# First expert's turned rows from an early gather of five tiles and one-hot products, in a decoder layer on one core

## What is computed

```python
x = x + merged @ w_out[l]
h2 = rms_norm(x, norm2_g[l])
x = x + hier_moe(h2, ...)
...
gl = (hf @ w_gr + b_gr)                     # 4 groups
g_idx = jnp.argmax(gl, axis=-1)
el = (hf @ w_er + b_er).reshape(N, N_GROUPS, EXPERTS_PER_GROUP)
top_v, top_i = lax.top_k(el_sel, TOP_K)     # 2 of the 8 experts of the group
w = jax.nn.softmax(top_v, axis=-1) * p_g[:, None]
...
a = xb @ w_gate[eid]
u = xb @ w_up[eid]
(jax.nn.silu(a) * u) @ w_down[eid]          # for each expert, on the rows that chose it
out = jnp.zeros((N, D)).at[row_tok].add(ys * row_w[:, None])
```

## Time and profile before

| | before |
|---|---|
| median of 3 runs | 1482.31 us (1481.53 to 1482.49) |
| the profiled execution: its time | 1481.47 us |
| the profiled execution: its span | 1479.7 us |
| TensorE busy | 1424.3 us, 96% of the span |
| VectorE, ScalarE, GpSimd busy | 1008.1, 828.9, 407.7 us |
| granted TensorE clock, mean | 0.99 |
| DMA, mean | 194 GB/s; 375 to 396 GB/s from slice 25 of 40 to slice 39 |

### The profile page before, as it was taken

The page is one execution under the profiler, slowest core; times in us unless marked ns, Lnnn a source line. Parts: engine busy times, 40 slices in busy tenths (PEclk is TensorE's granted clock), DMA queues, the critical chain, the costliest instruction groups (busy, mean ns, idle before and its releaser), DMA issues.

```text
span 1479.7 us, 19519 instructions
## 1 busy us (share of the span) xinstructions
PE 1424.3 (96%) x7296; PEld 1199.5 (81%) x7297; DVE 1008.1 (68%) x1444; ACT 828.9 (56%) x1342; POOL 407.7 (28%) x462
## 2 busy tenths in 40 slices
PE   5899999999999999999999979999999999999996
PEld 5788888888888788888888867888888888888885
DVE  6855664664574533344332567999999999999996
ACT  5653453353353322233232227888888888888883
POOL 3225424424433400000000011233333333333331
PEclk9999999999999999999999988999999999999999
DMA  7010110210210143354330549999999999999992
GB/s 220 23 44 12 51 44 1 62 43 1 61 44 0 44 115 99 86 149 121 91 142 36 198 152 385 375 386 385 392 386 387 386 389 389 393 396 393 389 384 89
DMA packets 134032, 286.39 MB, mean 194 GB/s; under 512 B 18864, under 2 KB 97840, under 8 KB 109360
## 3 DMA queue, kind: packets, MB, share of 16 engines
q1 hardware_dynamic: 119216, 263.79, 49.3%
q0 software_dynamic: 13248, 21.00, 3.8%
q10 hardware_dynamic: 1472, 0.32, 0.1%
HBM read 287.16 MB, written 25.17 MB: 211 GB/s over the span
## 4 chain that ended last, share of the span: by engine, by line
PE 85%; DMA 4%; DVE 4%; ACT 2%; POOL 2%; issue 2%; POOLq 0%; DVEq 0%; ACTq 0%
PE proj L105 17%; PE proj L107 16%; PE proj L106 16%; PE scores L105 6%; PE scores L107 6%; PE scores L106 6%; DMA w_slot<-in_w_up 4%; PE outs L760 2%; PE scores L693 2%; PE scores L571 1%; PE turned L105 1%; PE turned L107 1%; PE turned L106 1%; PE outs L851 1%; DVE w_low L1747 1%
## 5 line engine op out<-in xcount | busy, mean ns | idle before, releaser
L1747 DVE TENSOR_TENSOR w_low<-w_slot,w_high 128x2048 fp32r<-128x2048 f32 x192 | 430.9, 2285 | 0.1
L1186 ACT ACTIVATE w_high<-w_slot 128x2048 fp32r<-128x2048 f32 x190 | 352.6, 1907 | 20.1 <-DMA w_slot<-in_w_up 8.5
L105 PE MATMUL proj<-w_high,xeH 128*128 128x512 f32 x512 | 203.8, 398 | 3.9 <-DVE xeL L1850 1.9
L107 PE MATMUL proj<-w_high,xeL 128*128 128x512 f32 x512 | 200.6, 392 | 0.0
L106 PE MATMUL proj<-w_low,xeH 128*128 128x512 f32 x512 | 200.1, 391 | 0.0
L1376 POOL DMA_INDIRECT out<-y,ids_rows x31 | 86.5, 2791 | 342.8 <-DVE y L1860 342.8
L999 ACT ACTIVATE wCH<-wC_in 128x1024 fp32r<-128x1024 f32 x48 | 47.6, 1052 | 154.1 <-DMA wC_in<-in_w_branch_b 154.1
L1442 DVE TENSOR_TENSOR wCL<-wC_in,wCH 128x1024 fp32r<-128x1024 f32 x48 | 56.9, 1237 | 92.3 <-ACT wCH L999 92.3
L105 PEld LDWEIGHTS proj<-w_high,xeH 128*128 128x128 f32 x512 | 97.0, 189 | 25.5 <-issue 3.7
L107 PEld LDWEIGHTS proj<-w_high,xeL 128*128 128x128 f32 x512 | 96.5, 188 | 20.9
L106 PEld LDWEIGHTS proj<-w_low,xeH 128*128 128x128 f32 x512 | 96.7, 189 | 19.2
(11 more groups left out here) (299 smaller groups left out, 3167.4 us busy)
## 6 DMA issues: line engine op xcount, KB each, us to landing
w_slot<-in_w_gate SPq DMA_DIRECT2D x64, 1024.0 KB, 11.1
w_slot<-in_w_up SPq DMA_DIRECT2D x64, 1024.0 KB, 11.2
w_slot<-in_w_down SPq DMA_DIRECT2D x64, 1024.0 KB, 11.7
wC_in<-in_w_in SPq DMA_DIRECT2D x32, 512.0 KB, 4.8
wB_in<-in_w_in SPq DMA_DIRECT2D x16, 512.0 KB, 6.1
wA_in<-in_w_in SPq DMA_DIRECT2D x12, 512.0 KB, 5.9
x_all<-in_x SPq DMA_DIRECT2D x4, 1024.0 KB, 8.8
wC_in<-in_w_branch_a SPq DMA_DIRECT2D x16, 256.0 KB, 5.7
```

The lines of the kernel that those rows point to most:

```text
L105: pe.matmul(out, lh, rh, start=start, stop=False)
L107: return pe.matmul(out, ll, rh, start=False, stop=stop)
L1186: act.activation(w_high[slot][:], w_in6[slot][:], ACT.Copy).then_inc(S["w_split"], 1)
L1747: dve.tensor_tensor(w_low[slot][:], w_in6[slot][:], w_high[slot][:].bitcast(F32), ALU.subtract).then_inc(S["w_lows"], 1)
```

## The change

`first_ids`: when the positions of tiles 0 to 4 are known, their part of the table of rows is summed on its own. VectorE keeps it (in `w_rows`) and writes the first expert's column as `first_ids`. GpSimd gathers these rows of the first five tiles into `xe1`, ahead of its work on the norm of tile 6, as soon as the first five tiles are stored. Rows of later tiles stay zero there.

`first_pick`: for tiles 5, 6 and 7 VectorE writes a one-hot of the position within the first expert (`first_hot`; `far` moves tokens of other experts out of range). TensorE multiplies slices of `x2` with it (`first_late`), adds the early rows by products with the identity (`first_early`), and so has the first expert's turned rows in two PSUM banks without a full gather. VectorE scales them (`first_scaled`), ScalarE copies the first four slices one by one, and the first piece's products wait for each slice (`low_of`).

Moved: `picks` of tiles 5 to 7 and the last `rows_of` go behind the first slices and the first weight piece (`last_rows` on TensorE); the tables, and with them the gathers of `xe0` and `xe1`, come after that. `top_group` has six operations in place of seven. The third weight piece is split within the projection (ScalarE behind half 11, VectorE behind tile 2's placing), the fourth behind the second half's copy. `first_sq` keeps its place ahead of pieces 4 and 5, and now waits for the later gather. SyncE issues pieces 4 to 7 without a hold, and 8 and 9 once `x2` is no longer read.

```diff
@@ SyncE
             load_piece(3)
             store_x2(N_TILES - 1)
-            sp.wait_ge(S["xe_landed0"], DMA)
             for q in range(4, 6 * N_EXP):
                 if q == 8:
-                    sp.wait_ge(S["x2_stored"], N_TILES * DMA)
-                    sp.wait_ge(S["out_stored"], N_TILES * DMA)
+                    sp.wait_ge(S["x0_T"], 2)
+                    sp.wait_ge(S["early_stored"], 2 * N_EARLY * DMA)
+                    sp.wait_ge(S["late_stored"], 2 * (N_TILES - N_EARLY) * DMA)
                 load_piece(q)
@@ TensorE
+            def first_late(t, ks):
+
+                pe.wait_ge(S["place_step"], FIRST_HOT[t])
+                for k in ks:
+                    last = pe.matmul(first_turned(k), x2[:, t, DS(k, 128, step=8)], first_pick[t - N_EARLY][:, :],
+                                     start=(t == N_EARLY and k % 4 == 0), stop=(t == N_TILES - 1 and k % 4 == 3))
+                return last
+
+            def first_early(ks):
+
+                pe.wait_ge(S["xe_landed1"], DMA)
+                for k in ks:
+                    pe.matmul(first_turned(k), xe[1][:, DS(k, 128, step=8)], ident, start=False, stop=False)
+
+            first_late(5, range(4))
             turn_half(15)
+            first_late(5, range(4, 7))
+            positions_of(6)
             route_half(15)
-            positions_of(6)
-            rows_of(5)
+            first_early(range(4))
+            first_late(6, range(4))
+            first_late(5, [7])
+            first_early(range(4, 8))
             positions_of(7)
-            rows_of(6)
-            rows_of(7)
...
+            first_late(6, range(4, 6))
+            first_late(7, range(4)).then_inc(S["x0_T"], 1)
+            first_late(6, range(6, 8))
+            first_late(7, range(4, 8)).then_inc(S["x0_T"], 1)
...
-            pe.wait_ge(S["xe_landed0"], DMA)
-            for half, done in ((0, "x0_T"), (1, "xeT_done")):
-                for k in range(4 * half, 4 * half + 4):
-                    last = pe.transpose(SC[:, 0, k * 128:(k + 1) * 128], xe[0][:, DS(k, 128, step=8)], ident)
-                last.then_inc(S[done], 1)
@@ ScalarE
-                if cnt in (9, 10):
+                if cnt in (9, 10, 11):
                     high(w_high[cnt - 9][:], w_in6[cnt - 9][:], S[f"w_land{cnt - 9}"], DMA, S["w_split"])
...
-            high_piece(2)
+            act.wait_ge(S["xs_done"], 4)
+            for k in range(4):
+                act.activation(xeH[:, k, :], xs[:, k, :], ACT.Copy).then_inc(S["x0_H"], 1)
+            act.wait_ge(S["xs_done"], 8)
+            act.wait_ge(S["route_step"], R_DIFFS)
+            act.activation(xeH[:, 4:8, :], xs[:, 4:8, :], ACT.Copy).then_inc(S["xeH_done"], 1)
             high_piece(3)
-            act.wait_ge(S["route_step"], R_DIFFS)
...
             act.wait_ge(S["xe_landed0"], DMA)
+            act.wait_ge(S["rows_mm"], 9)
             act.activation(first_sq[:], xe[0][:], ACT.Square, scale=1.0 / 32, accum_out=first_ms[:]).then_inc(S["first_sum"], 1)
@@ GpSimd
             for i in range(N_TILES):
+                if i == N_EARLY + 1:
...
+                    pool.wait_ge(S["early_stored"], 2 * N_EARLY * DMA)
+                    pool.wait_ge(S["tables_done"], 1)
+                    pool.indirect_dma_start(out=xe[1][:], out_offset=None, in_=x2_dram[0:N_EARLY * 128, :],
+                                            in_offset=bass.IndirectOffsetOnAxis(ap=first_ids[:, 0:1], axis=0),
+                                            bounds_check=N_EARLY * 128 - 1, oob_is_err=False).then_inc(S["xe_landed1"], DMA)
@@ VectorE
+            def first_hot(t):
+
+                dve.wait_ge(S["pos_mm"], t + 1)
+                place(dve.scalar_tensor_tensor(first_pick[t - N_EARLY][:], pos_bank(t)[:, 0:1].to_broadcast([P, 128]),
+                                               far[:, t - N_EARLY:t - N_EARLY + 1], const("iota", 0, 128), ALU.add, ALU.is_equal))
...
+                if i == 7:
+                    first_hot(5)
+                    place_rows(5)
                 add_residual(1, i)
...
+                if i == 6:
+                    dve.wait_ge(S["rows_mm"], N_EARLY)
+                    route(dve.tensor_scalar(w_rows[:, 0:32], bank(3)[:, 0:32], float(NO_ROW), None, ALU.add))
+                    row_ids(first_ids[:], bank(3)[:, 0:1], "tables_done")
```

More of the change, by code:

```diff
@@ L32 @@
 DMA = 16
[L35 removed]
+R_DIFFS, R_WEIGHTS = 86, 103
 NO_ROW = 1024
@@ L38 @@
 N_GROUPS = 4
+NO_SLOT = 4096.0
+N_EARLY = 5
+PLACED = {t: 2 * t + 2 + max(t - N_EARLY + 1, 0) for t in range(N_TILES)}
+FIRST_HOT = {t: PLACED[t] - 2 for t in range(N_EARLY, N_TILES)}
 def expert_at(j):
@@ L305, in decoder_layer @@
         r_rows = rs("r_rows", [P, 256])
+        first_pick = [sb(f"first_pick{i}", [P, 128], F32, at=R_WORK + 16 * KIB + (i + 1) * KIB + 512) for i in range(3)]
         rc = region(merged_at[1] + 16 * KIB, merged_at[1] + 16 * KIB + 1152)
@@ L1221, in _ @@
             act.wait_ge(S["xe_landed0"], DMA)
+            act.wait_ge(S["rows_mm"], 9)
             act.activation(first_sq[:], xe[0][:], ACT.Square, scale=1.0 / 32, accum_out=first_ms[:]).then_inc(S["first_sum"], 1)
-            act.wait_ge(S["first_sum"], 2)
-            for half, turned, done in ((0, "x0_T", "x0_H"), (1, "xeT_done", "xeH_done")):
-                ks = slice(4 * half, 4 * half + 4)
-                x_scaled(turned, 1, range(4 * half, 4 * half + 4), None)
-                act.wait_ge(S["xs_done"], 4 * half + 4)
-                act.activation(xeH[:, ks, :], xs[:, ks, :], ACT.Copy).then_inc(S[done], 1)
             for c in (0, 1):
@@ L1747, in low_piece, with row_ids, first_scaled @@
                 dve.tensor_tensor(w_low[slot][:], w_in6[slot][:], w_high[slot][:].bitcast(F32), ALU.subtract).then_inc(S["w_lows"], 1)
+            def row_ids(table, rows, done):
+                dve.tensor_scalar(table, rows, float(NO_ROW), None, ALU.add).then_inc(S[done], 1)
+            def first_scaled(half):
+                ks = slice(4 * half, 4 * half + 4)
+                dve.wait_ge(S["x0_T"], half + 1)
+                dve.tensor_tensor(xs[:, ks, :], bank(6 - half).rearrange("p (k c) -> p k c", k=4),
+                                  g2x[:, ks].unsqueeze(2).to_broadcast([P, 4, 128]), ALU.mult).then_inc(S["xs_done"], 4)
             for i in range(N_TILES):
@@ L1844, in hid_low @@
                                   high_[:].rearrange("p a b -> p (a b)").bitcast(F32), ALU.subtract).then_inc(S["hidL_done"], 1)
-            low_piece(2)
-            for half, ready, done in ((0, "x0_H", "x0_L"), (1, "xeH_done", "xeL_done")):
-                dve.wait_ge(S[ready], 1)
-                ks = slice(4 * half, 4 * half + 4)
-                dve.tensor_tensor(xeL[:, ks, :], xs[:, ks, :], xeH[:, ks, :].bitcast(F32), ALU.subtract).then_inc(S[done], 1)
             low_piece(3)
@@ L1865, in last_rows @@
                 dve.wait_ge(S[f"again_landed{e % 2}"], DMA * ((e - N_GROUPS) // 2 + 1))
-                for half, done in ((0, "y_half"), (1, "y_out")):
+                for half in range(2):
                     cols = slice(half * 512, half * 512 + 512)
```

141 lines of the change are left out of this document (87 added, 54 removed).

## The result

| | before | after |
|---|---|---|
| median, 4 runs each on one chip | 1482.40 us (1481.53 to 1482.73) | 1492.78 us (1491.30 to 1494.11) |
| ratio | | 1.0066, 95% interval 1.0054 to 1.0078 |
| profiled execution: time, span | 1481.47, 1479.7 us | 1492.45, 1490.2 us |
| first weight product of the first expert | 891.93 us | 895.03 us |
| first product of the second expert | 910.47 us | 920.16 us |

The forecast was 1482.9 us (1478.0 to 1489.0): the time lies above the range. Of the 10.5 us in the span, 3.1 are there when the first expert starts and 9.7 when the second does.

What follows compares the result with a forecast made beforehand. TensorE's queue plus its holes was taken to bound the kernel, with the weight stream nearly as long. Second expert late (+2.7) and late weights gone (−2.1) gave +0.6 us on 1482.31: 1482.9 us, range 1478.0 to 1489.0.

Steps and rivals of the forecast that it cites:

- Step 1: Third weight piece split inside the projection: ScalarE waits for it, TensorE's queue slips by 0.9 us.
- Step 2: Early gather on GpSimd ahead of tile 6's norm: norm at 875.1, last residual at 877.4, 4.8 us late.
- Step 3: One-hot products on TensorE: 0.11 us a pass, clock back at 880.8, first weight product at 888.2 instead of 891.93.
- R2: TensorE at the low clock, first in the one-hot stretch, second behind the gather wait: +4 to +8 us, chance 0.22.
- Step 4: Lists written after the first expert's start; late gathers take 8.7 and 10.8 us; second expert at 913.2, 2.7 us late.
- Step 5: From the second expert to the end: weights flow since 879, so the 2.1 us of late weights go.
- R1: Late gathers land quickly (4.7 and 5.7 us): end 4.0 us earlier, 1478.3 us; chance 0.17.
- R3: Loaded late gathers are slower still, 11 to 12 us: +3 to +4 us, 1486 us; chance 0.15.

Runs made afterwards that it cites:

- b2: Kernel before with only the third weight piece split within the projection: ratio 0.9997 (0.9988 to 1.0007) to the kernel before.
- a2: Changed kernel with the early gather on GpSimd behind tile 6's norm instead of ahead of it: ratio 1.0053 to the kernel before.
- a1: Changed kernel with the slices loaded for one-hot and identity products being 128 neighbouring columns, not every eighth: ratio 1.0027 to the kernel before.
- a3: Changed kernel with nothing waiting for the first expert's gathered rows and the second expert's gather issued first: ratio 1.0048 to the kernel before.
- c1: Changed kernel with weight piece 8 and what follows held until both late gathers have landed: ratio 1.0034 to the kernel before.
- b1: Kernel before with only the hold of weight pieces behind the gather taken away: ratio 1.0030 to the kernel before.
- v1: New version of the change: one-hot loaded, x2's rows as 512 moving columns, no late gather for the first expert, pieces 6 on held: ratio 0.9963 to the kernel before.
- w1: Kernel before with 40 products that nobody reads put into TensorE's hole: ratio 0.9986 to the kernel before.
- d1: Changed kernel with the edits of a1, a2 and c1 together: ratio 0.9994 (0.9985 to 1.0003) to the kernel before.
- v1b: v1 with the hold of weight piece 6 and what follows taken away: ratio 0.9959 to the kernel before.

## Why the prediction was wrong

**Step 1, the third piece: right as a mechanism, too small to matter.** ScalarE's waiting row is there (852.02, 5.64 us idle, the turned copy at 854.45). The slip of 0.9 us was 0.1 in the profiled execution; b2 shows it in full (0.86 us). In the whole time neither can be seen.

**Step 2, the norm held by the early gather: right.** Predicted: norm at 875.1, last residual at 877.4; measured 874.61 (874.04 and 0.57) and 877.04. The early rows landed in 7.1 us, not 4.7, and were not late. a2 prices the hold at 2.2 us of S.

**Step 3, the price of a pass: the step that failed.** The prediction took 0.11 us from L903 and put the first weight product at 888.2; it came at 895.03, 6.8 us later. Two terms were mis-sized. The row at L903 has contiguous columns; the new passes load every eighth one and cost 0.23 at full clock. The prediction took them as the same operation because both are plain f32 products, and did not look at the access pattern. That is worth 4.2 us in F (a1). The other: the clock was expected back at 880.8 and was 0.50 up to 886, so the first half of the passes would have cost 0.21 even with contiguous columns. That is R2, and holds most of the remaining 2.6 us: in a1 the 26 passes between the routing products and the positions of tile 7 took 4.6 us (882.36 to 886.93) where the prediction had 2.9. Whether the clock comes back early or late is not fixed by this code, as a3 shows, so this term could have gone either way; the step of the columns costs at either level. With the first alone the sum would have been 1487.1, with both 1489.7: slower, not the same.

**Step 4, the lists behind the start: right, in its size partly by luck.** Predicted: the second expert 25.0 us behind the first product, ScalarE and TensorE waiting for gathers of 8.7 and 10.8 us. Measured: 25.1, with 10.0 and 10.6. c1 confirms the mechanism. Two errors nearly cancel: the list was written 3.8 us behind the first product and not 4.8, and the first late gather then held GpSimd for 3.1 us and not 1.6, so the second was issued 7.8 us behind and not 7.3. And the loaded landings were taken over from rows, but the hold whose removal brings them was not priced as a part of the change: with it back S comes 4.5 us earlier (c1), and b1 shows that its removal costs 4.4 us even without the rest.

**Step 5, late weights disappear: wrong.** Predicted −2.1 us. The last expert's turns came 10.4 us later than before and the second expert 9.7, so 0.7 more was lost in between, not 1.7 less, and the wait of 0.4 stayed. The 0.7 can't be told from none: from the third expert's turns to the last expert's, 29 periods, the profiled executions lose between 1.6 us (before) and 3.7 (b2), and b2 has the steady part of the kernel before unchanged. What is shown is that nothing came back. Weights flowed 9 us earlier, but DMA was empty (0.00 of share at 916 to 918) before the steady part began; from there the landings grow from 7.6 (925 to 945) to 18 in both kernels. The tail is 569 to 573 us in all runs, whatever the start. An early start of a ring of ten slots fills the ring and no more.

**The sum.** +0.6, then +7.0 (step 3, and 0.1 of step 4) and +2.9 (step 5, of which 2.1 were claimed as gain) make 10.5, the difference of the spans. **The rivals:** R1 and R3 fell (10.0 and 10.6 us), R2 happened in its first place in this execution, together with the step of the columns, which none of the rivals had. In its second place 32 products took 4.3 us of the 4.5 expected.

## What to carry to other kernels

A duration is carried from a row to a new instruction only if its access pattern is the same: for operands that TensorE loads, look at the step of the columns and at the granted clock of the stretch, and put the strided operand on the other side of the product where that is possible. A gather that someone waits for should not share the DMA with bulk loads that nobody waits for yet; a hold at that one place cost nothing that these runs can measure and was worth about what the landing grows by (c1, b1). When a wait is moved rather than removed, follow every list, gather and square that now comes behind it up to the next point where all engines meet, and compare there.

## What the runs showed of the hardware

- A plain f32 pass of 128 columns costs TensorE 0.12 us at full clock with contiguous loaded columns and 0.23 with a step of 8 (load 192 and 335 ns); at the low clock it costs 0.21 and 0.26. A pass of 512 moving columns costs 0.47 to 0.48 at full clock (v1).
- The granted clock stayed at 0.50 up to 886, though TensorE had been at work since 876.56; in a3, with the same instructions up to there, it was back 3.6 us after they began. In w1 it was 0.50 from 882 to 884, in the midst of 24 products that ran back to back. In v1 it fell behind two holes of 1.8 us and 1.2 us with short waits between them.
- A gather of 128 rows on GpSimd's queue takes 4.4 to 6.1 us to land with the DMA idle or running dry (v1, d1, w1, c1 and the kernel before), and 8.7 to about 11 while 1 MB pieces keep flowing (v1b, b1, the changed kernel and the earlier trace rows). The Trainium skill, "DMA: Bandwidth & Descriptors", section "Queues, rings and completion order", has each DMA engine take turns between queues, packet by packet; c1 shows that this does not shield the gather here: the same gather took 10.6 us with weights and 4.8 without.
